# A decoder block on one Trainium2 core: the two parts of the MLP's tokens are stored side by side

## What is computed

```python
    h = h + m @ w_out[l]
    u = rmsnorm(h, ffn_norm_w[l])
    a = causal_dwconv(u @ w_ffn_gate[l], ffn_conv_w[l], ffn_conv_b[l])
    h = h + (jax.nn.silu(a) * (u @ w_ffn_up[l])) @ w_ffn_down[l]
return rmsnorm(h, final_norm_w)[:, N_META:]
```

## Time and profile before

| what | us |
|---|---|
| median of 3 runs | 1578.09 |
| lowest and highest | 1577.22, 1578.19 |
| the profiled execution, its own time | 1577.4 |
| its span in the trace | 1575.7 |
| TensorE busy with matmuls | 1564.5 |
| VectorE, ScalarE, GpSimd busy | 1010.4, 705.8, 147.1 |

### The profile page before, as it was taken

The page is one execution under the profiler, slowest core; times in us unless marked ns, Lnnn a source line. Parts: engine busy times, 40 slices in busy tenths (PEclk is TensorE's granted clock), DMA queues, the critical chain, the costliest instruction groups (busy, mean ns, idle before and its releaser), DMA issues.

```text
span 1575.7 us, 28471 instructions
## 1 busy us (share of the span) xinstructions
PE 1564.5 (99%) x11780; PEld 1472.0 (93%) x11780; DVE 1010.4 (64%) x1225; ACT 705.8 (45%) x744; POOL 147.1 (9%) x218
## 2 busy tenths in 40 slices
PE   9999999999999999999999999999999999999998
PEld 8999999999999999999999999998888999998886
DVE  7655788843355566696777677775446777776453
ACT  7433555544433345653445545544333344444342
POOL 1000150000000002247540000000000000000000
PEclk9999999999999999999999999999999999999999
DMA  7755555655565553578777655555546565656451
GB/s 251 224 177 164 159 179 182 191 185 172 186 201 165 161 161 120 173 252 222 209 216 254 197 175 185 188 180 194 198 177 210 163 207 165 196 177 220 181 214 54
DMA packets 264237, 294.64 MB, mean 187 GB/s; under 512 B 23914, under 2 KB 249419, under 8 KB 263763
## 3 DMA queue, kind: packets, MB, share of 16 engines
q1 hardware_dynamic: 238146, 278.78, 54.4%
q0 software_dynamic: 4000, 8.45, 1.9%
q10 hardware_dynamic: 22016, 6.33, 1.7%
HBM read 285.12 MB, written 8.42 MB: 186 GB/s over the span
## 4 chain that ended last, share of the span: by engine, by line
PE 90%; issue 3%; ACT 2%; DVE 2%; POOL 1%; DMA 1%; ACTq 0%; SPq 0%; DVEq 0%; POOLq 0%
PE ps L679 19%; PE ps L680 18%; PE ps L681 18%; PE ps L1095 10%; PE ps L1137 5%; PE ps L1135 5%; PE ps L1138 5%; PE ps L1093 5%; ACT w_hi L1179 2%; PE ps L1089 1%; POOL x_sh L631 1%; PE ps L818 0%; DVE xt L1847 0%; PE ps L859 0%; DVE w_lo L1499 0%
## 5 line engine op out<-in xcount | busy, mean ns | idle before, releaser
L1499 DVE TENSOR_TENSOR w_lo<-raw,w_hi 128x2048 fp32r<-128x2048 f32 x259 | 595.3, 2299 | 310.6 <-ACT w_hi L1179 310.2
L1179 ACT ACTIVATE w_hi<-raw 128x2048 fp32r<-128x2048 f32 x259 | 495.6, 1915 | 542.6 <-PE ps L681 238.2
L679 PE MATMUL ps<-u_hi,w_hi 128*128 128x258 f32 (+1 forms) x1528 | 442.6, 290 | 0.0
L680 PE MATMUL ps<-u_lo,w_hi 128*128 128x258 f32 (+1 forms) x1528 | 435.0, 285 | 0.0
L681 PE MATMUL ps<-u_hi,w_lo 128*128 128x258 f32 (+1 forms) x1528 | 433.8, 284 | 0.0
L679 PEld LDWEIGHTS ps<-u_hi,w_hi 128*128 128x128 f32 x1528 | 287.5, 188 | 5.4 <-DVE z_qf L1612 2.5
L681 PEld LDWEIGHTS ps<-u_hi,w_lo 128*128 128x128 f32 x1528 | 287.9, 188 | 0.0
L680 PEld LDWEIGHTS ps<-u_lo,w_hi 128*128 128x128 f32 x1528 | 287.7, 188 | 0.3
L1095 PE MATMUL ps<-u_all,w_hi 128*128 128x512 f32 x660 | 233.7, 396 | 0.0
L679 PE MATMUL ps<-u_all,w_hi 128*128 128x258 f32 x704 | 198.9, 283 | 0.0
L681 PE MATMUL ps<-u_all,w_lo 128*128 128x258 f32 x704 | 198.8, 282 | 0.0
(11 more groups left out here) (314 smaller groups left out, 1908.2 us busy)
## 6 DMA issues: line engine op xcount, KB each, us to landing
raw<-in_w_in_dram SPq DMA_DIRECT2D x47, 2048.0 KB, 8.4
raw<-in_w_ffn_gate_dram SPq DMA_DIRECT2D x22, 2048.0 KB, 8.0
raw<-in_w_ffn_up_dram SPq DMA_DIRECT2D x22, 2048.0 KB, 8.0
raw<-in_w_ffn_down_dram SPq DMA_DIRECT2D x20, 2048.0 KB, 7.9
raw<-in_w_out_dram SPq DMA_DIRECT2D x8, 2048.0 KB, 10.3
raw<-in_w_branch_hgrn_dram SPq DMA_DIRECT2D x8, 1024.0 KB, 5.5
raw<-in_w_branch_dsa_dram SPq DMA_DIRECT2D x8, 1024.0 KB, 9.0
gate_spill<-gate_st ACTq DMA_DIRECT2D x32, 129.0 KB, 3.8
```

Source lines behind the costliest of these rows:

```text
L679: mm(acc, w_hi[s][:, k, :], mov_hi(k), start=(k == first), stop=False)
L680: mm(acc, w_hi[s][:, k, :], mov_lo(k), start=False, stop=False)
L1179: activation(w_hi[m % 4][:], raw[(m // 2) % 2][:, :, P * (m % 2):P * (m % 2) + P], ACT.Copy)\
L1499: v.tensor_tensor(w_lo[m % 4][:], raw[(m // 2) % 2][:, :, P * (m % 2):P * (m % 2) + P], w_hi[m % 4][:].bitcast(F32), ALU.subtract).then_in ...
```

## The change

The low part of a block's tokens now lies right behind its high part: `u2_all` is [128, 16, 516]. In the low part the order is turned, so that its first two tokens come last. Tokens 2 to 257 of the high part and then of the low part are one run of 512 columns, which an up unit moves (lines 1105 and 1111 of the changed kernel). In a gate unit the low part goes to columns 2 to 259 of the bank, two further than the high part: tokens 2 to 257 fall on their own columns, and the sums of the low part's first two tokens land in columns 258 and 259. So that these columns are opened, the first block's high tokens come from a copy with two zero columns behind it (`u2_first`, 260 columns). VectorE then adds these two sums to the first two columns.

```diff
@@ -120,8 +120,9 @@
         UA = 98304
         u_hi = at("u_hi", UA, [P, KT, T], F32R)
         u_lo = at("u_lo", UA + 17408, [P, KT, T], F32R)
-        u2_all = at("u2_all", UA, [P, 2, KT, TQ], F32R)
-        u2_hi, u2_lo = u2_all[:, 0, :, :], u2_all[:, 1, :, :]
+        u2_all = at("u2_all", UA, [P, KT, 2 * TQ], F32R)
+        u2_hi, u2_lo = u2_all[:, :, 0:TQ], u2_all[:, :, TQ:2 * TQ]
+        u2_first = at("u2_first", UA + 33024, [P, TQ + 2], F32R)
         R = [133120 + ZB * j for j in range(9)]
         m_hi = at("m_hi", R[0], [P, KT, TQ], F32R)
         m_lo = at("m_lo", R[0] + 16512, [P, KT, TQ], F32R)
@@ -196,6 +197,7 @@
         h_sq = at("h_sq", R[7] + 640, [P, TQ])
         ssq = at("ssq", R[7] + 1672, [P, TQ])
         h_rs = at("h_rs", R[7] + 2704, [P, TQ])
+        g_last = [at(f"g_last{a}", UA + 34064 + 8 * a, [P, 2]) for a in range(2)]
         g_raw = [at(f"g_raw{a}", BIAS + 1032 * a, [P, TQ]) for a in range(2)]
         up_parts = at("up_parts", BIAS + 4096, [P, 2, SEQ])
         hid_hi = at("hid_hi", R[0], [P, FH, SEQ], F32R)
@@ -1078,21 +1080,35 @@
             for half, (u_ff, u_down) in enumerate(((U_FF, U_DOWN), (U_FF2, U_DOWN2))):
 
                 def gate(u, ks, half=half, u_ff=u_ff):
-                    ins = products(ps[4 * half + u][:, 0:TQ], (u_ff + u) % 4, ks, *tokens(0, u2_hi, u2_lo, TQ))
+                    s, acc = (u_ff + u) % 4, ps[4 * half + u]
+                    for k in ks:
+                        if k == 0:
+                            mm(acc[:, 0:TQ + 2], w_hi[s][:, k, :], u2_first[:], start=True, stop=False,
+                               skip_group_check=True)
+                        else:
+                            mm(acc[:, 0:TQ], w_hi[s][:, k, :], u2_hi[:, k, :], start=False, stop=False,
+                               skip_group_check=True)
+                        if k < KT - 1:
+                            mm(acc[:, 2:TQ + 2], w_hi[s][:, k, :], u2_lo[:, k, :], start=False, stop=False,
+                               skip_group_check=True)
+                        ins = mm(acc[:, 0:TQ], w_lo[s][:, k, :], u2_hi[:, k, :], start=False, stop=(k == KT - 1),
+                                 skip_group_check=True)
+                        if k == KT - 1:
+                            ins = mm(acc[:, 2:TQ + 2], w_hi[s][:, k, :], u2_lo[:, k, :], start=False, stop=True,
+                                     skip_group_check=True)
                     if ks[-1] == KT - 1:
                         ins.then_inc(projected, 1)
 
                 def up(u, half=half, u_ff=u_ff):
 
                     s, acc = (u_ff + u) % 4, ps[4 * half + u]
-                    both = acc[:].rearrange("p (a t) -> p a t", a=2)
-                    mm(both, w_hi[s][:, 0, :], u2_all[:, :, 0, 2:TQ], start=True, stop=False, skip_group_check=True)
+                    mm(acc[:], w_hi[s][:, 0, :], u2_all[:, 0, 2:2 * TQ - 2], start=True, stop=False, skip_group_check=True)
                     mm(acc[:, 0:SEQ], w_lo[s][:, 0, :], u2_hi[:, 0, 2:TQ], start=False, stop=False,
                        skip_group_check=True)
                     for k in range(1, KT):
                         mm(acc[:, 0:SEQ], w_lo[s][:, k, :], u2_hi[:, k, 2:TQ], start=False, stop=False,
                            skip_group_check=True)
-                        ins = mm(both, w_hi[s][:, k, :], u2_all[:, :, k, 2:TQ], start=False, stop=(k == KT - 1),
+                        ins = mm(acc[:], w_hi[s][:, k, :], u2_all[:, k, 2:2 * TQ - 2], start=False, stop=(k == KT - 1),
                                  skip_group_check=True)
                     ins.then_inc(projected, 1)
 
@@ -1434,6 +1450,8 @@
 
             for u in range(16):
                 act.wait_ge(out_free, u + 3)
+                if u == 0:
+                    activation(u2_first[:, 0:TQ], h_res[:, u, :], ACT.Copy, scale=vec_a[:, V_FFN + u:V_FFN + u + 1])
                 activation(u2_hi[:, u, :], h_res[:, u, :], ACT.Copy, scale=vec_a[:, V_FFN + u:V_FFN + u + 1])\
                     .then_inc(u2h_ready, 1)
                 ahead(U_OUT + u + 1)
@@ -1850,8 +1868,13 @@
                 v.tensor_tensor(h[:, 0:2], ps[6 + u % 2][:, 0:2], xm[:, u, 0:2], ALU.add)
                 v.tensor_tensor(h[:, 2:TQ], ps[6 + u % 2][:, 2:TQ], xt[u % 2][:], ALU.add).then_inc(out_free, 1)
                 dve.wait_ge(u2h_ready, u + 1)
-                v.scalar_tensor_tensor(u2_lo[:, u, :], h, vec_a[:, V_FFN + u:V_FFN + u + 1], u2_hi[:, u, :].bitcast(F32),
-                                       ALU.mult, ALU.subtract).then_inc(u2l_ready, 1)
+                if u == 0:
+                    v.memset(u2_first[:, TQ:TQ + 2].bitcast(F32), 0.0)
+                for lo, hi in ((0, 2), (2, TQ)):
+                    ins = v.scalar_tensor_tensor(u2_lo[:, u, (lo - 2) % TQ:(lo - 2) % TQ + hi - lo], h[:, lo:hi],
+                                                 vec_a[:, V_FFN + u:V_FFN + u + 1], u2_hi[:, u, lo:hi].bitcast(F32),
+                                                 ALU.mult, ALU.subtract)
+                ins.then_inc(u2l_ready, 1)
                 if u >= 4:
                     dve.wait_ge(h_out[u % 4], 64 * (u // 4))
                 v.transpose(h_sh[u % 4][:], h[:, 2:TQ]).then_inc(h_turned, 1)
@@ -1892,7 +1915,9 @@
                             tap = lambda vec, c: vec[:, ds(2 * i + (c + FH * half + u), 1)]
                             c = conv[u][:]
                             g = g_raw[u]
+                            v.tensor_tensor(g_last[u][:], ps[4 * half + u][:, TQ:TQ + 2], h_rs[:, 0:2], ALU.mult)
                             link(v.tensor_tensor(g[:], ps[4 * half + u][:, 0:TQ], h_rs[:], ALU.mult))
+                            v.tensor_tensor(g[:, 0:2], g[:, 0:2], g_last[u][:], ALU.add)
                             link(v.tensor_scalar(c, g[:, 2:TQ], tap(vec_c, V_C2), tap(vec_a, V_CB),
                                                  ALU.mult, ALU.add))
                             link(v.scalar_tensor_tensor(c, g[:, 1:TQ - 1], tap(vec_b, V_C1), c, ALU.mult, ALU.add))
```

## The result

The changed kernel takes 1580.63 us (median of 17 runs, 1580.39 to 1581.32), the kernel before, run beside it, 1577.79 us (17 runs). The ratio is 1.0019, with a 95% interval of 1.0012 to 1.0026: **slower by 2.8 us**, where 2.9 us less were forecast. It lies outside the range, and no rival had both this size and this place.

A forecast was written before the change was run, and what follows sets the result against it. TensorE, busy nearly throughout at full clock, was taken as the bound. Terms of -3.3 (up units), +0.04 (gate units) and +0.4 us (head of the MLP) made -2.9: 1575.2 us from 1578.09, range 1573.0 to 1577.3.

The forecast's parts named there:

- What one run of 512 costs: Up units: the big product steps 226.8 ns, as in down units, not 231.5; 4.7 ns less, 704 times, -3.3 us.
- the bound that I gave for no gain: Up units: least gain is nothing, if the 4.7 ns come from the change between short and long products.
- The bounds: Up units: the gain from joining the two runs lies between nothing and 4.9 us (7 ns a pair).
- The step that put the shifted write at nothing: Gate units: low products writing from column 2 of the bank cost nothing, as up units' reads from two columns in.
- The sentence on the Trainium skill's "SBUF Cachelines" section: Up units, big product: lines touched are 130 or 128 in turn before, 129 after joining; no gain on the mean.
- The forecast of the gate units: Gate units on TensorE: 5.76 us as before, 0.04 us in all for 260 columns in place of 258.
- the slower rival: Gate units: low products' shifted write costs TensorE, at 12 ns each ending at 1583.6 us; chance 0.05.
- The head of the MLP: OUT, unit 0: one more rounding on ScalarE delays the last sum and TensorE by 0.41 us; +0.4 us, once.
- the ring: OUT: sum, `u2_hi`, `w_hi` on ScalarE, `w_lo` on VectorE, next sum; 15 rounds of 5.64 us, without slack.
- The cover: Gate units: VectorE's added 0.2 to 0.3 us each is hidden, with 14.5 us for the bank, 12.7 for `w_lo`.
- The split of `u2_lo` and the memset: OUT, VectorE: the split's 0.08 to 0.16 us a unit and the memset lie in its 0.96 us wait.
- The rival "gain nothing": Up units gain nothing, the excess coming from alternating lengths; only the head's 0.4 us is left, 1578.5 us; chance 0.12.

The follow-up runs named there:

- old_off16: The kernel before, still two runs of 256, with rows of 260 columns in place of 258 and the tile moved by 8 bytes: 1574.43 us, ratio 0.9981.
- two_runs: Probe on the changed kernel: the 512-column product of up units made of two separate runs of 256, one on a 16-byte line, one off: 1579.88 us.
- lines_a: Probe on the changed kernel: gate products read 256 columns, from column 0 in the first half, from column 2 in the second: 1578.21 us.
- shape: Changed kernel with rows moved 8 bytes; 512 columns cut into 2, then 4 neighbouring runs, gate low products written from column 0, then 2: 1575.27 us.
- old_off8: The kernel before, still two runs of 256, with rows of 260 columns in place of 258, all runs off a 16-byte line: 1581.85 us, ratio 1.0028.
- row64: The changed kernel with rows of 2112 bytes, the run of 512 columns beginning on a multiple of 64 bytes: 1576.27 us, ratio 0.9993.

## Why the prediction was wrong

**The step that failed: "What one run of 512 costs".** I took 231.5 ns for the big product of an up unit and 226.8 for a down product, and put the 4.7 ns between them down to the second run. The second run is not what costs: `old_off16` has two and is at 347.7 ns a pair, under both kernels with one run on a line, and `two_runs` is no dearer than the changed kernel. Two runs are dearer only where both are off a line, 356.4 against 354.5 ns, with one line more to touch. What the difference holds is, first, the blocks that were off a line: 3.2 ns of 350.9, the step to 347.7. What is left when all are on a line, 349.0 less the 118.1 of `lines_a`, is an estimated 230.9 ns for a run of 512 in an up unit, still 4 ns over a down product. So the bound that I gave for no gain, that short and long products in turn cost more than a stream of one length, is the nearest to what is left. No run here took it apart, and it stays open.

**The bounds ended at nothing.** I let the change of layout gain or do nothing for the up units, and had no bound for a loss. The step that put the shifted write at nothing says why: "up units read from two columns into a row without a price that shows". The price was there, in every second block, and a mean over all blocks can't show it. The loss lay in the rows' length, which I took only for its mean. The sentence on the Trainium skill's "SBUF Cachelines" section ("Advanced Engine Details and Errata") has it: two runs touched 130 or 128 lines in turn, one run touches 129. From this I concluded that there was no difference on the mean. The runs bear out that lines of 16 bytes matter (256 columns on 64 lines 118.1 ns, on 65 lines 120.4), but the count left out the 256-column product. The change doesn't touch its line of code, but it went from half its blocks off to all, and its mean duration from 279 to 283 ns. With both products counted, a pair touched 193.5 lines on the mean and now touches 194. At the fitted 2.6 ns a line that is 1.3 ns of the 3.6 by which a pair became dearer (350.9 to 354.5). So counting lines on the mean gives a loss, but about a third of it. For the rest, the kernel before lies 1.6 ns below what its lines give, and the changed one 0.7 above. What makes that difference stays open.

**The forecast of the gate units** (5.76 as before, 0.04 us for the 260 columns) missed 0.6 us. Of this I can only say what it isn't. `shape` frees the shifted write, the slower rival that I named. The gate units of `old_off8`, with neither a shift nor 260 columns, have 5.774 us, as the changed kernel's 5.775. Both have their high parts on a line in all blocks, but that isn't the cause by itself, since `row64` has them off a line and 5.777.

**The head of the MLP** (+0.4 us) was right in its mechanism and wrong in its sum. Unit 0's round of the ring took 6.34 us, 0.42 more than before, by the starts of the sum:

```profile
744.30 0.41 DVE L1869 TENSOR_TENSOR h_res<-ps,xt 128x256 f32<-128x256 f32 x1
...
750.64 0.41 DVE L1869 TENSOR_TENSOR h_res<-ps,xt 128x256 f32<-128x256 f32 x1
```

But the later rounds are all 5.56, and before three of the 15 were longer: the first, and two of 6.01 and 6.02, which were not in my rows since I counted one mean of 5.64. In both of these, `w_lo` took 2.75 or 2.76 us and not 2.29; the last of them, in the kernel before:

```profile
797.99 2.76 DVE L1499 TENSOR_TENSOR w_lo<-raw,w_hi 128x2048 fp32r<-128x2048 f32 x1 [0.96 <-ACT w_hi L1179]
```

Why these two are gone I can't say from these runs. Without them the ring ended 0.5 us earlier, and TensorE's wait of 0.5 us is gone.

**What was right.** VectorE is busy 11.5 us more, where 10 to 15 were forecast: its two new instructions last 160 and 162 ns, and TensorE waits for none of it. The cover stands. The split of `u2_lo` and the memset are hidden as said.

**The rival "gain nothing"** was the nearest, and had 0.12. It too kept the price of an up unit from rising.

## What to carry to other kernels

Where TensorE is busy all the time, as here, the start and the length of a row of the moving operand are part of its price. When a layout is changed, work out for every product that reads it, also those whose code stays, how many 16-byte lines each block touches before and after; rows of an odd number of 8-byte steps hide a bad start in half of the blocks, and a change that makes all blocks alike may make them all bad. A difference between two places of a kernel (up and down units here) doesn't price the one thing in which the change makes them equal: a probe that changes that thing alone would have shown it before.

## What the runs showed of the chip

- Moving 256 columns of this 4-byte type cost 118.1 ns from the start of a 16-byte line and 120.4 from 8 bytes into it, at the full granted clock, in a stream of products of the same length.
- In pairs of a 256- and a 512-column product, 348.6 ns for 192 lines and 2.6 for each line more (up to 195) fit ten measured prices within 0.9 ns. The kernel whose blocks alternate between 192 and 195 lines lies 1.6 ns below the fit.
- The same 32 products at the same addresses take 5.639 to 5.682 us, as the products ahead of them differ.
- Two runs of 256 cost no more than one of 512 where they touch as many lines (347.7 against 349.0 and 348.3 ns a pair with all on a line; 353.1 and 353.9 with one of the two off, against 354.5). With both off, one line more, they cost 2.0 ns more (356.4 against 354.5).
- A write that begins two columns further into a PSUM bank than those around it costs nothing here (5.743 and 5.744 us a gate unit).
